# Two blocks of a hybrid sequence model: gates of the gated linear attention made one pair of heads at a time, with the 1/16 as a scale on ScalarE, and the residual's stores split around weight loads

## What is computed

```python
g_log = log_sigmoid(ga @ gla_a2 + gla_a_b) / 16.0          # ga: rank 16, per key channel
# per chunk of 64 tokens, 4 heads of 64 key and 128 value channels
cum   = cumsum(g, axis=tokens)
o     = (q * exp(cum)) @ state + intra-chunk scores(q, k, exp(cum_i - cum_j)) @ v
state = exp(cum_last) * state + (k * exp(cum_last - cum)).T @ v
y_gla = rms_norm(o) * silu(gr)
```

## Time and profile before

| | |
|---|---|
| median of 3 runs | 2445.11 us (2441.11 to 2447.93) |
| the profiled execution | 2450.07 us, span 2448.4 us, mean granted TensorE clock 0.972 |
| TensorE busy | 2331.3 us, 95% |
| VectorE, ScalarE, GpSimd busy | 1033.4, 628.1, 1148.0 us |
| read from and written to HBM | 205.54 MB, 25.17 MB |

### The profile page before, as it was taken

One profiled execution on the slowest core, in us unless ns is written; L12 is line 12 of the kernel. 1 busy time (PEld: TensorE's weight loads), 2 busy tenths in 40 slices (PEclk: granted clock), 3 DMA queues, 4 the chain that ended last, 5 costly groups with the idle time before them and its releaser, 6 DMA issues.

```text
span 2448.4 us, 29287 instructions
## 1 busy us (share of the span) xinstructions
PE 2331.3 (95%) x11096; PEld 1876.1 (77%) x11096; DVE 1033.4 (42%) x1190; ACT 628.1 (26%) x720; POOL 1148.0 (47%) x1106
## 2 busy tenths in 40 slices
PE   5999996999889999999999999999999999999997
PEld 3777775787667877787777778877788888888885
DVE  6786555345641343153247524645633200232406
ACT  5453332244431222112113223224311000111111
POOL 2342230656541313222265234366666677666675
PEclk8999997999988999999999999999999999999999
DMA  4223333222421111111111124442423333333343
GB/s 175 85 72 126 120 120 129 89 88 81 148 68 44 43 44 52 60 35 61 44 44 52 52 92 140 146 159 88 157 95 100 97 103 103 95 101 95 111 155 121
DMA packets 68759, 231.92 MB, mean 95 GB/s; under 512 B 7345, under 2 KB 8513, under 8 KB 68673
## 3 DMA queue, kind: packets, MB, share of 16 engines
q1 hardware_dynamic: 65216, 218.15, 26.8%
q10 hardware_dynamic: 3456, 12.58, 1.3%
HBM read 205.54 MB, written 25.17 MB: 94 GB/s over the span
## 4 chain that ended last, share of the span: by engine, by line
PE 77%; issue 5%; DVE 5%; ACT 4%; POOL 3%; DMA 2%; DVEq 1%; POOLq 1%; ACTq 1%; SPq 1%
PE PG L573 33%; PE PG L657 15%; PE PG L610 13%; PE PG L1034 5%; POOL WL L493 2%; DMA WRAW<-down_w 1%; PE PX L762 1%; PE PX L999 1%; PE PX L758 1%; DVE PX L1669 1%; POOLq L492 1%; PE PX L689 1%; PE PG L1046 1%; PE PX L769 1%; PE PX L997 1%
## 5 line engine op out<-in xcount | busy, mean ns | idle before, releaser
L493 POOL TENSOR_TENSOR WL<-WRAW,WH 128x1024 fp32r<-128x1024 f32 (+2 forms) x304 | 700.5, 2304 | 45.1 <-issue 0.9
L490 POOL TENSOR_TENSOR TOUCH<-TOUCH 128x2 f32<-128x2 f32 x304 | 86.7, 285 | 1218.5 <-PE PG L657 455.6
L573 PE MATMUL PG<-UL,WH 128*128 128x512 f32 x1120 | 438.4, 391 | 0.0
L573 PE MATMUL PG<-UH,WH 128*128 128x512 f32 x1008 | 398.4, 395 | 10.2 <-POOL WL L493 7.8
L573 PE MATMUL PG<-UH,WL 128*128 128x512 f32 x1008 | 394.9, 392 | 0.0
L491 POOL TENSOR_SCALAR WH<-WRAW 128x1024 fp32r<-128x1024 f32 (+2 forms) x304 | 310.4, 1021 | 0.0
L573 PEld LDWEIGHTS PG<-UL,WH 128*128 128x128 f32 x1120 | 211.9, 189 | 45.5 <-issue 1.9
L657 PE MATMUL PG<-UH,WH 128*128 128x512 f32 x544 | 230.9, 425 | 3.8 <-POOL WL L493 3.8
L573 PEld LDWEIGHTS PG<-UH,WH 128*128 128x128 f32 x1008 | 190.8, 189 | 55.6 <-issue 11.6
L573 PEld LDWEIGHTS PG<-UH,WL 128*128 128x128 f32 x1008 | 190.5, 189 | 40.0
L657 PE MATMUL PG<-UL,WH 128*128 128x512 f32 x544 | 220.4, 405 | 0.0
(11 more groups left out here) (474 smaller groups left out, 3565.9 us busy)
## 6 DMA issues: line engine op xcount, KB each, us to landing
WRAW<-up_w SPq DMA_DIRECT2D x88, 512.0 KB, 3.5
ADA<-ada_w SPq DMA_DIRECT2D x24, 1024.0 KB, 5.8
WRAW<-down_w SPq DMA_DIRECT2D x48, 512.0 KB, 3.6
WRAW<-out_w SPq DMA_DIRECT2D x30, 512.0 KB, 3.6
WRAW<-zg_w SPq DMA_DIRECT2D x24, 512.0 KB, 3.5
gates<-STG ACTq DMA_DIRECT2D x24, 512.0 KB, 2.6
WK<-gates SPq DMA_DIRECT2D x24, 512.0 KB, 3.4
WRAW<-gla_w SPq DMA_DIRECT2D x18, 512.0 KB, 3.5
```

The costliest lines, as they stand in the source:

```text
L490: pool.tensor_tensor(TOUCH[:, 0:2], TOUCH[:, 2:4], TOUCH[:, 4:6], ALU.add)
L493: pool.tensor_tensor(WL[:, r, 0:n], WRAW[:, r, 0:n], WH[:, r, 0:n].bitcast(F32), ALU.subtract).then_inc(w_split, 1)
L573: mm = pe.matmul(PG[:, bank, :], w[:, r, P * k:P * k + P], v, start=first and k == 0 and n == 0, stop=last and k == kbs - 1 and n == 2)
```

## The change

- SP: two rounds, each of which loads one pair of gla0b's weights and then stores four of the eight blocks of H; the third pair follows.
- VectorE: bias and minimum are made for the first pair and signalled, then for the second, whose minimum goes to TMP instead of WK. The three clears follow, then the subtraction for the first pair alone (`gla_log`). The second pair's subtraction is made by the callback after the second group of states of i = 0. The two multiplications by 1/16 are removed.
- ScalarE: `load_exp`, an Exp of one element per partition into a new column `scratch`, is added behind the copy of miscb. Then `gla_softplus` (Exp, Ln) for the first pair, then the copy of keys and queries, then `load_exp` once more. `gla_softplus` for the second pair stands behind the two `gate_out` of i = 0, in front of `la_rest`. The five exponentials of the GLA pairs have the scale 1/16 or -1/16.
- VectorE waits for `slot_free` of unit 0 before it multiplies the queries of i = 0.

```diff
--- before.py
+++ after.py
@@ -41,7 +41,7 @@
 ]
 
 VEC_MADE = [
-    ("zero", 1), ("eps", 1), ("one", 1), ("rg_s8", 4), ("neg_rg_s8", 4), ("lb", 4), ("one_minus_lb", 4), ("tmp", 24),
+    ("zero", 1), ("eps", 1), ("one", 1), ("rg_s8", 4), ("neg_rg_s8", 4), ("lb", 4), ("one_minus_lb", 4), ("tmp", 24), ("scratch", 2),
     ("pre1_g", 8), ("post1_g", 8), ("pre2_g", 8), ("post2_g", 8),
 ]
 
@@ -388,11 +388,13 @@
             for name in ("gatea", "gateb", "misca", "gla0a", "miscb"):
                 for i in range(TILE0_PAIRS[name]):
                     weight_pair(name, i)
-            sp.wait_ge(h2_made, KB)
-            for j in range(KB):
-                sp.dma_start(h_save[j * P:(j + 1) * P, :], H[:, j, :]).then_inc(h_saved, 16)
+            for i in range(2):
+                weight_pair("gla0b", i)
+                sp.wait_ge(h2_made, KB)
+                for j in range(4 * i, 4 * i + 4):
+                    sp.dma_start(h_save[j * P:(j + 1) * P, :], H[:, j, :]).then_inc(h_saved, 16)
             for name in ("gla0b", "zg0", "gla1", "zg1"):
-                for i in range(TILE0_PAIRS[name]):
+                for i in range(2 if name == "gla0b" else 0, TILE0_PAIRS[name]):
                     weight_pair(name, i)
             for i in range(3):
                 weight_pair("ml0", i)
@@ -1223,15 +1225,19 @@
             def half_row(s, k):
                 return WK[:, s, 512 * k:512 * k + 512].rearrange("p (n c) -> p n c", c=32)
 
-            def la_exps(la, i, b, bm, eb, ek, ed):
+            def load_exp():
+
+                act.activation(vec("scratch", 0), vec("one"), ACT.Exp)
+
+            def la_exps(la, i, b, bm, eb, ek, ed, unit=1.0):
 
 
                 act.wait_ge(la["gaps"], i + 1)
-                act.activation(WK[:, ed, :], WK[:, ed, :], ACT.Exp)
-                act.activation(WK[:, eb, :], WK[:, b, :], ACT.Exp)
-                act.activation(half_row(bm, 1), half_row(bm, 0), ACT.Exp)
-                act.activation(halves(ek, True), halves(b, True), ACT.Exp, scale=-1.0)
-                act.activation(halves(ek, False), half_row(bm, 0), ACT.Exp, scale=-1.0).then_inc(la["exps"], 1)
+                act.activation(WK[:, ed, :], WK[:, ed, :], ACT.Exp, scale=unit)
+                act.activation(WK[:, eb, :], WK[:, b, :], ACT.Exp, scale=unit)
+                act.activation(half_row(bm, 1), half_row(bm, 0), ACT.Exp, scale=unit)
+                act.activation(halves(ek, True), halves(b, True), ACT.Exp, scale=-unit)
+                act.activation(halves(ek, False), half_row(bm, 0), ACT.Exp, scale=-unit).then_inc(la["exps"], 1)
 
             def la_turned(la, i, n_turn, dst):
 
@@ -1390,15 +1396,18 @@
                 split_high(1, j, 32, MOD[:, j:j + 1])
             gla0_copy("gla0a", 0, 2)
             misc_copy("miscb", 1)
+
+            def gla_softplus(b, x):
+
+                act.wait_ge(gla_x, b + 1)
+                act.activation(x, x, ACT.Exp)
+                act.drain()
+                act.activation(x, x, ACT.Ln, bias=vec("one")).then_inc(gla_ln, 1)
+
+            load_exp()
+            gla_softplus(0, WK[:, 11, :])
             gla0_copy("gla0b", 1, 0)
-
-            act.wait_ge(gla_x, 1)
-            for b in range(2):
-                act.activation(WK[:, 11 + b, :], WK[:, 11 + b, :], ACT.Exp)
-            act.drain()
-            for b in range(2):
-                act.activation(WK[:, 11 + b, :], WK[:, 11 + b, :], ACT.Ln, bias=vec("one")).then_inc(gla_ln, 1)
-
+            load_exp()
 
             def gate_out(q, n, t):
 
@@ -1416,7 +1425,7 @@
                     act.wait_ge(tile_done, t + 1)
                     act.activation(WK[:, 4, :], slot(0), ACT.Copy).then_inc(slot_free[0], 1)
                 act.wait_ge(gl["free"], i + 1)
-                la_exps(gl, i, 2, 9, 12, 13, 10)
+                la_exps(gl, i, 2, 9, 12, 13, 10, 1.0 / 16)
                 if i == 0:
                     gla0_copy("gla0b", 1, 1)
                     gla0_copy("gla0b", 1, 2)
@@ -1430,6 +1439,8 @@
                 la_turned(gl, i, 3, [5, 6, 10])
                 for n in range(2):
                     gate_out(2 * i + n, n, TILE0[f"zg{i}"] + n)
+                if i == 0:
+                    gla_softplus(1, TMP[:, 0, :])
                 if i:
                     act.wait_ge(m["rows"], 1)
                     act.activation(WK[0:4, 1, :], WK[0:4, 1, :], ACT.Exp)
@@ -1996,21 +2007,26 @@
             h2_split(1, 0, 8)
 
             dve.wait_ge(gla_a2, 1)
-            for b in range(2):
+            for b, x in ((0, WK[:, 11, :]), (1, TMP[:, 0, :])):
                 dve.tensor_scalar(WK[:, b, :], aux(2 * b), vec("gla_a_b", b), None, ALU.add)
-            dve.drain()
-            for b in range(2):
-                dve.scalar_tensor_tensor(WK[:, 11 + b, :], WK[:, b, :], -1.0, WK[:, b, :], ALU.mult, ALU.min)
-            dve.drain().then_inc(gla_x, 1)
+                dve.drain()
+                dve.scalar_tensor_tensor(x, WK[:, b, :], -1.0, WK[:, b, :], ALU.mult, ALU.min)
+                dve.drain().then_inc(gla_x, 1)
             dve.memset(WK[:, 14, :], 0.0)
             dve.memset(WK[:, 16, :], 0.0)
             dve.memset(WK[:, 17, 0:P], 0.0)
-            for b in range(2):
+
+            def gla_log(b, x):
+
                 dve.wait_ge(gla_ln, b + 1)
-                dve.scalar_tensor_tensor(WK[:, b, :], WK[:, b, :], 0.0, WK[:, 11 + b, :], ALU.min, ALU.subtract)
-            dve.drain()
-            for b in range(2):
-                dve.tensor_scalar(WK[:, b, :], WK[:, b, :], 1.0 / 16, None, ALU.mult)
+                dve.scalar_tensor_tensor(WK[:, b, :], WK[:, b, :], 0.0, x, ALU.min, ALU.subtract)
+                dve.drain()
+
+            def gla_second_log(n):
+                if n == 2:
+                    gla_log(1, TMP[:, 0, :])
+
+            gla_log(0, WK[:, 11, :])
             dve.wait_ge(h_saved, 16 * KB)
             dve.drain().then_inc(gl["free"], 1)
             def tiles(x):
@@ -2059,13 +2075,16 @@
                 la_gaps(gl, 2, 9, 10, WK[:, ds(i, 1), :].rearrange("p a t -> p (a t)"))
                 dve.drain()
                 dve.wait_ge(gl["exps"], i + 1)
+                if i == 0:
+                    U = UNIT0["gla0b"]
+                    dve.wait_ge(slot_free[U % 2], U // 2 + 1)
                 dve.tensor_tensor(WK[:, 11, :], WK[:, 3, :], WK[:, 12, :], ALU.mult)
                 dve.tensor_tensor(half_row(9, 0), chunks(3)[:, :, 32:CH], half_row(9, 1), ALU.mult)
                 U = UNIT0["gla1"] + 3 if i else UNIT0["gla0b"] + 1
                 dve.wait_ge(slot_free[U % 2], U // 2 + 1)
                 dve.tensor_tensor(WK[:, 10, :], WK[:, 4, :], WK[:, 10, :], ALU.mult).then_inc(gl["kd"], 1)
                 dve.tensor_tensor(WK[:, 13, :], WK[:, 4, :], WK[:, 13, :], ALU.mult).then_inc(gl["keys"], 1)
-                la_core(gl, i, 2, 64, [14, 16], 17, 12, ml_rows if i else None)
+                la_core(gl, i, 2, 64, [14, 16], 17, 12, ml_rows if i else gla_second_log)
                 for hh in range(2):
                     dve.wait_ge(gl["rs"], i * 2 + hh + 1)
                     dve.scalar_tensor_tensor(WK[:, 3, :], aux(0), vec_at("gla_norm_w", i * 2 + hh), WK[:, 2, :],
```

## The result

| | before | changed |
|---|---|---|
| median | 2443.11 us (4 runs, 2440.55 to 2447.93) | 2416.05 us (4 runs, 2414.19 to 2421.66) |
| ratio | | 0.9885, 95% interval 0.986 to 0.991 |
| profiled execution, span | 2450.07, 2448.4 us | 2421.66, 2419.9 us |
| mean granted clock | 0.972 | 0.982 |

The change makes the kernel 27 us faster, where 16 were forecast, outside the stated range. Up to the first filler (the first piece of the next weights' products, behind the transposes) the mechanism was right but for one dip of the clock, worth 3 us. The other 9 us of the two profiles came behind it. Both profiled executions are slow ones of their kernels: that of the kernel before is longer than the four runs of the table, that of the changed kernel is the longest of its four.

What follows compares the result with a forecast made beforehand. TensorE was taken as the bound, so gains come only where it stands still or runs slowly. Terms 4.2 + 1.7 + 9.4 + 1.3 − 0.6 = 16.0 us, off a median of 2445.11, gave 2429.1 us; range 2422 to 2436.

Steps and rivals of the forecast that it cites:

- The first hole: TensorE's wait before gla0b's first product: 5.24 us shrinks to 1.0, 4.2 gained, plus 1.7 from its tile at full clock.
- the bound taken: Gla0b's second pair, issued behind the first half of the stores, lands by 675.3 even at the loaded 6.82 us.
- The dip behind L833: Low clock on gla0b's second tile, 8.21 us instead of 5.49: taken as unchanged, nothing gained.
- the first rival: The dip behind L833 goes too, as TensorE no longer stops before gla0b: 2426.4 us, chance 10%.
- The second hole: TensorE's wait before the transposes, for the key product of L2066: all 9.4 us gained.
- VectorE's chain: Gate work leading to the key product of L2066, in the new order: product done at 701.3.
- Its cover: Key product ready 6.1 us before TensorE comes to the transposes.
- The transposes: 24 transposes behind the second hole take 3.27 us instead of 4.54, 1.3 gained.
- The cost taken on: Splits TensorE needs end late beside VectorE's chain: 0.6 us lost, bounds 0 and 3.6.
- Behind ScalarE: Second pair's Exp, Ln and two loads, 4.7 us, fit ScalarE's 12.59 us idle before L1246's square, 7.9 spare.
- The step that failed: Behind the transposes, later work and waits follow TensorE, so the whole 16.0 us shift reaches the end.

Runs made afterwards that it cites:

- e1: Kernel before with only the new SP order, H stores split around gla0b's weights: 2435.23 us, ratio 0.9954.
- h2: Changed kernel plus seven extra dense products (1.6 us) behind the S5 stage: 2417.97 us, ratio 0.9906 to the kernel before.
- g4: Changed kernel without both early table loads and with the 1/16 multiplication back on VectorE: 2424.59 us, one execution.
- e3: Kernel before with only the 1/16 as a scale of ScalarE's exponentials, VectorE's two multiplications removed: 2439.99 us, ratio 0.9972.

## Why the prediction was wrong

**The first hole**: right. 0.94 us for 1.0; the tile kept its clock, 1.5 us gained for 1.7; the gla0b tile landed under the stores within the bound taken, 674.2 for 675.3.

**The dip behind L833**: a mis-sized term. The sum kept it, at nothing gained; the changed kernel lost it, 2.5 us on the tile and 0.7 on the small matmuls. This was the first rival at 10%, and its reason (no stop of TensorE in front of gla0b) fits the traces. All seven profiles with the first hole, whatever else was in them, have the second tile at 8.0 to 8.4 us, while of the eleven without it nine have 5.6 and two 7.2 (`e1` and `h2`): it went mostly, not always. The argument against it, that ten microseconds lay between, was no evidence: only one case was at hand.

**The second hole**: right, and so was VectorE's chain: the key product at 701.5 for 701.3. Its cover was 3.4 us, not 6.1, because TensorE came 2.5 us earlier. The transposes take 3.3 us, as forecast. The cost taken on, 0.6, was 0.53, by one split of the shape named.

**Behind ScalarE**: covered, with 4.2 us left instead of 7.9. TensorE came to the square 3.1 us sooner behind the last `gate_out` (12.59 to 9.47 us), most of it by its clock, and the moved work took 5.3 us with its start, not 4.7.

**The step that failed** is "What follows is TensorE's own work and waits relative to it, so the shift should reach the end." It put at nothing what the clock does behind the filler. Waits are relative; the clock isn't. The 670 us behind the first filler alternate dense products with groups of small matmuls and short stops. Some of these are met by a low stretch, and which ones changes when all are moved by a microsecond or so, and also from one execution to the next. The kernel before happened to stand badly: by the ratios this gave the changed kernel 6 to 7 us (mean of three comparisons, 3 to 9), and 9 in the two profiles. With the 3.2 us of the dip, that is nearly all that the forecast lacked. The runs support this: with equal delays in both kernels the gain is 12 to 26 us, mean 19, and seven products more in front of the filler gave either sign. The range failed for the same reason. It took the spread of three runs, 6.8 us, for all that the clock can do; 22 runs on another chip spread from 2435.06 to 2451.81, and their mean clocks from 0.981 to 0.971.

What stays open: why the clock falls at one place and not at another 1 us on, and why two executions of one kernel differ in it. I haven't tried to work out its rule, and no version was sought that stands well on purpose.

## What to carry to other kernels

Price a removed stop of TensorE with the slow products around it, on both sides. Where dense products alternate with small ones, a shift of a microsecond or two can redraw the low stretches behind it; here that moved the ratio by up to 0.3%, so a difference of that size between two kernels says little about the edit. Put the same delay in front of that work in both kernels, at three or four sizes, and compare the means; and read the direct gain in the trace at the last point that is still before it.

## What had not been expected

More work made the kernel faster: seven matmuls of 0.23 us in front of the first filler took the kernel before from 2446.97 to 2435.15 us (medians; ratio 0.9971, which is 7 us). The mean granted clock went from 0.975 to 0.979 with it (medians of the runs).

A multiplication of 128x1024 by a constant took 0.69 us on VectorE alone (`g4`) and 2.2 beside GpSimd (4.34 for two, before). When the chain was shortened (`e3`), the same conflict moved from L1819 to L1817 and L2061 and took back 2.4 of 4.5 us.
